# A two-block transformer kernel: eight-slot ring for expert matrices, one block for router and experts, combine inside the layers

## Chip, cores and metric

The kernel runs on one core of a Trainium2 chip. The metric is the device time of one execution in microseconds. TensorE is the matrix engine, VectorE (DVE), ScalarE (ACT) and GpSimd (POOL) are the others; SyncE (SP) only issues DMAs. Each engine executes its own program in order and the engines meet through semaphores. Everything is computed in float32.

## What is computed

The input is `x` with 512 tokens of 1024 features. The first block is a mixer (dilated attention, retention, gates) and a mixture of 64 experts, of which each token uses two; the second block has two layers of attention, pooling, a gated memory and a feed-forward part. The reference, cut to what the change touches:

```python
def first_block(x, ...):
    h = x
    xn = rms_norm(h, norm_mix_w[0])
    h = h + hybrid_mixer(xn, ...)
    hn = rms_norm(h, norm_moe_w[0])
    h = h + hierarchical_moe(hn, w_group, b_group, w_expert, b_expert, w1, w3, w2)
    return rms_norm(h, norm_final_w)

def hierarchical_moe(x2, ...):
    group_p = softmax(x2 @ w_group + b_group);  g_w, g_idx = top_k(group_p, 1)
    sel = (x2 @ w_expert + b_expert) of the chosen group
    e_w, e_idx = top_k(softmax(sel), 2);  e_w = e_w / sum(e_w)
    gate = g_w * e_w;  eid = g_idx * 8 + e_idx
    # every token and choice is put into a slot of its expert
    hid = silu(xb @ w1[e]) * (xb @ w3[e])         # 1024 -> 512
    y = hid @ w2[e]                               # 512 -> 1024
    return sum over both choices of gate * y

def second_block(x, ...):
    h = layer_norm(x, ln0_g, ln0_b)
    for l in range(2):
        h = layer_norm(ALPHA * h + mix(h), ...)
        h = layer_norm(ALPHA * h + conv_glu_ffn(h), ...)
    return h
```

The matrices w1, w3 and w2 of one expert have 2 MB each, 64 experts 403 MB.

## The kernel before

The program is a row of blocks. A block has one instruction stream per engine, and all engines meet at its end: load of x, norm, mixer, merge, a block that clears semaphores (`give_back`), norm (`norm_block`), router (`router_block`), experts (`moe_block`), combine (`combine_block`), another `give_back`, and the layers (`layers_block`) of the second part. All SBUF memory is one tensor `arena`; `mixer_memory`, `moe_memory` and `layer_memory` lay views of it over one another.

Mixer: SP issues four small table loads (`tables_in`), then nine loads of w_in, three for each of three slots (`sp_first`, L277), each of 512 KB in pieces of 512 bytes, then the attention masks. The first matmul (L328) waits for the three loads of slot 0. POOL waits for `tables_in` and then starts with a memset.

Norm before the experts: SP loads the norm's weights, ACT squares, POOL takes the power, DVE scales, PE transposes (L786), ACT copies to `aT` (L717).

Router: SP loads the router's matrices, biases and four constant tables (L957), with `rw_in` counting all eight; POOL writes 4 MB of zeros to the DRAM buffer `y_slots` (L996), the rows of possible overflow blocks. PE multiplies `aT` with the router matrices (L977, 64 matmuls of 72 columns). DVE then runs a chain of some hundred small instructions, each waiting for the one before, that ends in the slot number `yrel` of each token and choice (L1095), its integer form for the combine (L1098 to L1100), and the number of overflow blocks, which goes to DRAM and back through SP (L967, L969). With these inputs no overflow block is needed.

Experts: each expert has 32 slots for tokens. A loop of 16 turns handles four experts per turn, as two pairs. Six SBUF slots of 2 MB hold w1, w3 of two experts and w2 of two experts. For each pair PE waits for the four up matrices, issues 64 up matmuls (L1183, four at a time in the four column groups), four transposes (L1189), waits for the two w2 and issues 32 down matmuls (L1199). ACT applies silu (L1252) and copies the transposed hidden values (L1254); DVE multiplies (L1304) and copies the result out (L1309); ACT sends it to `y_slots` (L1257). SP fetches the next up matrices after `up_done` (L1137, L1138) and the next w2 after `down_done` (L1143). At the end of each turn PE gathers the tokens of the next four experts by 64 matmuls with a 0/1 matrix `G` (L1165), which DVE has made by comparing `yrel` with a ramp (L1288 twice, then L1294 or L1301), and ACT copies them to `xt` (L1244). The gather is also done after the last turn.

Combine: POOL issues 16 indirect DMAs (L1340), each fetching half a result row (2 KB) for 128 tokens and one of their two choices; DVE adds each, times the gate, to `h` (L1353). After `give_back` the layers begin: SP loads weights (L2302 on, L1692), ACT squares `h` (L2329), DVE and POOL make the norm's factor, DVE applies it (L2385), and the second part follows.

## Time and profile before

| | us |
|---|---|
| median of 3 runs | 3744.47 |
| lowest and highest run | 3734.27, 3748.82 |
| profiled execution | 3744.31 |
| its span, first to last instruction | 3742.5 |
| PE busy | 3031.5 (81%) |
| DVE busy | 680.5 (18%) |
| ACT busy | 508.1 (14%) |
| POOL busy | 278.2 (7%) |

Busy PE time is modelled, since matmuls are pipelined, and the granted clock of TensorE changes in the run. The page has the span in 40 equal slices of 93.6 us. The other views are: the waits (who waited for whom), the timeline (instructions in order of time with the idle time ahead of each and what ended it), windows (busy time, granted clock and DMA of a stretch), and the DMA view (packets and bytes of each queue).

### The profile page before, as it was taken

The page shows a single profiled execution, that of the slowest core. Times are in us where ns is not written, and L with a number is a line of the kernel's source. Part 1 is how long each engine was busy: PE and PEld are TensorE (multiplying, and loading weights), DVE is VectorE, ACT ScalarE, POOL GpSimd, SP SyncE. Part 2 cuts the span into 40 slices and gives each one's busy share as a digit, 9 for nine tenths or more (in the row PEclk, how much of TensorE's full clock was granted, in tenths as well). Part 3 has the DMA queues.
Part 4 walks back from the last instruction along what each step waited for, and adds up shares of the span by engine and source line. Part 5 has one row for each costly group of instructions (what it writes and reads, how often), then busy time and mean ns, then how long its engine had stood idle before and what let it go on. Part 6 is the DMA issues. An engine that isn't in the chain of part 4 may idle for free. (4 is left out here: it accounts for less than half of the span.)

```text
span 3742.5 us, 30146 instructions
## 1 busy us (share of the span) xinstructions
PE 3031.5 (81%) x12308; PEld 1589.1 (42%) x12308; DVE 680.5 (18%) x1742; ACT 508.1 (14%) x1001; POOL 278.2 (7%) x283
## 2 busy tenths in 40 slices
PE   6999999999645555545455559899999998999999
PEld 4666665544531222212122235444444554444443
DVE  1222222201120100000010032331110222321102
ACT  1222242210100000000000021310000113210000
POOL 1000003211000000000000040020000200020000
PEclk9999999999857778777787779999999998999999
DMA  5111111113149999999999841112312111032220
GB/s 151 51 34 51 34 35 51 57 34 101 58 172 394 388 387 395 389 391 398 395 386 387 344 149 59 57 45 68 101 68 79 58 69 57 5 98 89 68 90 34
DMA packets 193092, 587.06 MB, mean 157 GB/s; under 512 B 16994, under 2 KB 143202, under 8 KB 168162
## 3 DMA queue, kind: packets, MB, share of 16 engines
q1 hardware_dynamic: 186066, 568.93, 39.6%
q0 software_dynamic: 2320, 8.39, 0.7%
q10 hardware_dynamic: 4608, 8.39, 0.6%
q8 instruction: 67, 1.10, 0.1%
q14 instruction: 31, 0.25, 0.0%
HBM read 571.00 MB, written 14.68 MB: 156 GB/s over the span
## 5 line engine op out<-in xcount | busy, mean ns | idle before, releaser
L1183 PE MATMUL bank<-arena 128*32 128x512 f32 x2048 | 297.5, 745 | 416.6 <-DMA arena<-in_moe_w 416.6
L2238 PE MATMUL bank<-arena 128*128 128x512 f32 (+2 forms) x1472 | 608.6, 576 | 9.1 <-DVE arena L1627 9.1
L328 PE MATMUL bank<-arena 128*128 128x384 f32 x1280 | 431.1, 489 | 14.5 <-DMA arena<-in_w_in 14.5
L2238 PEld LDWEIGHTS bank<-arena 128*128 128x128 f32 x1472 | 275.9, 191 | 339.8 <-issue 329.7
L1183 PEld LDWEIGHTS bank<-arena 128*32 128x32 f32 x2048 | 81.5, 133 | 621.1 <-issue 621.1
L328 PEld LDWEIGHTS bank<-arena 128*128 128x128 f32 x1280 | 237.4, 190 | 175.5 <-DMA arena<-in_w_in 14.8
L2247 PE MATMUL bank<-arena 128*128 128x512 f32 x704 | 303.2, 592 | 0.0
L1741 PE MATMUL bank<-arena 128*128 128x512 f32 (+3 forms) x736 | 249.7, 499 | 0.0
L2247 PEld LDWEIGHTS bank<-arena 128*128 128x128 f32 x704 | 133.0, 189 | 168.4 <-issue 168.4
L1741 PEld LDWEIGHTS bank<-arena 128*128 128x128 f32 x736 | 139.1, 190 | 104.1 <-issue 72.6
L1304 DVE TENSOR_TENSOR arena<-bank,arena 64x512 f32<-64x512 f32 x32 | 32.8, 1026 | 689.3 <-ACT arena L1252 689.3
L1165 PE MATMUL bank<-arena 128*128 128x128 f32 x1088 | 128.6, 279 | 25.0 <-DVE arena L1294 25.0
L1199 PE MATMUL bank<-arena 128*32 128x512 f32 x1024 | 130.6, 655 | 15.2 <-ACT arena L1254 15.2
L1165 PEld LDWEIGHTS bank<-arena 128*128 128x128 f32 x1088 | 125.4, 195 | 38.6 <-DVE arena L1294 25.2
L1252 ACT ACTIVATE arena<-bank 64x512 f32<-64x512 f32 x32 | 18.9, 591 | 750.5 <-PE bank L1183 750.5
L1916 PE MATMUL bank<-arena 128*128 128x512 f32 x256 | 111.4, 592 | 0.0
L325 PE MATMUL bank<-arena 128*128 128x512 f32 x256 | 110.9, 593 | 0.0
L2289 DVE TENSOR_SCALAR arena<-arena 128x512 f32<-128x512 f32 x44 | 25.3, 574 | 457.9 <-ACT arena L2275 457.9
L1340 POOL DMA_INDIRECT arena<-y_slots,arena x16 | 17.4, 1090 | 1136.9 <-PEq L1334 1132.3
L2275 ACT ACTIVATE arena<-bank 128x512 f32<-128x512 f32 x44 | 26.3, 598 | 522.9 <-PE bank L2238 522.9
L389 PE MATMUL bank<-arena 128*128 128x64 f32 x640 | 81.0, 275 | 12.3 <-ACT arena L453 12.3
L1661 POOL TENSOR_TENSOR arena<-arena 128x1 f32<-128x1 f32 x20 | 13.0, 648 | 995.7 <-DVE arena L1639 995.7
(304 smaller groups left out, 2676.0 us busy)
## 6 DMA issues: line engine op xcount, KB each, us to landing
arena<-in_moe_w SPq DMA_DIRECT2D x192, 2048.0 KB, 19.0
arena<-in_w_up SPq DMA_DIRECT2D x44, 1024.0 KB, 7.7
arena<-in_w_in SPq DMA_DIRECT2D x52, 512.0 KB, 5.6
arena<-in_w_down SPq DMA_DIRECT2D x10, 2048.0 KB, 7.7
arena<-in_w_in SPq DMA_DIRECT2D x12, 1024.0 KB, 5.2
y_slots<-arena ACTq DMA_DIRECT2D x32, 256.0 KB, 9.9
arena<-in_w_in SPq DMA_DIRECT2D x4, 2048.0 KB, 9.8
arena<-in_w_out SPq DMA_DIRECT2D x4, 2048.0 KB, 7.8
```

The lines of the kernel that those rows point to most:

```text
L325: ins = pe.matmul(banks[s % 2][:, :], w[:, k, tile(b)], m.aT[:, k, :], start=(k == 0), stop=(k == KT - 1))
L328: ins = pe.matmul(banks[s % 2][:, 0:CW], m.aT[:, k, tile(t)], w[:, k, :], start=(k == 0), stop=(k == KT - 1))
L389: ins = pe.matmul(banks[2][:, 256:256 + HD], m.pt[:, tile(4 * i + j)], m.v[q % 2][:, k, g, HD * hh:HD * hh + HD], start=(i == 0 and j == 0 ...
L1165: ins = pe.matmul(banks[5 + d // 4][:, tile(d % 4)], m.hn[:, t, tile(d)], m.G[:, t, :], start=(t == 0), stop=(t == T - 1))
L1183: ins = pe.matmul(banks[pr][q:q + CAP, :], m.xt[:, k, c:c + CAP], up_dst(2 * e2 + up)[:, k, :], start=(k == 0), stop=(k == KT - 1))
L1199: ins = pe.matmul(banks[3 + pr][q:q + CAP, :], m.ht[:, f, CAP * e2:CAP * e2 + CAP], down_dst(4 + e2)[:, f, 512 * half:512 * half + 512], s ...
L1304: dve.tensor_tensor(by_place(m.hid[0:64, :], FF // P), spread(banks[pr][64:128, :], FF // P), spread(m.hs[64:128, :], FF // P), ALU.mult)\
L1741: ins = pe.matmul(out, a, b, start=(i == 0), stop=(i == len(terms) - 1))
L1916: ins = pe.matmul(banks[2 * t + half][:, :], m.mixT[:, k, tile(t)], slot_view(m, i)[:, k, :], start=(first and k == ks[0]), stop=(last and ...
L2238: ins = pe.matmul(banks[2 * (j % 2) + half][:, part], w[:, k, c0:c0 + P], m.aT[:, k, part], start=(k == 0), stop=(k == KT - 1))
L2247: ins = pe.matmul(banks[2 * t + half][:, :], m.hidT[:, k, tile(t)], v[:, k % 4, 512 * half:512 * half + 512], start=(k == 0), stop=(k == N ...
L2275: act.activation(m.gp[j % 2][:, 2:], banks[2 * (j % 2) + 1][:, :], ACT.Copy).then_inc(G["f_gcopy"], 1)
```

## The change

1. `y_slots` is laid out in rows of 1024 values, one row per slot, instead of two rows of 512. The write of 4 MB of zeros moves from the router block to the start of `pool_mixer`, behind the wait for `tables_in`; POOL's first write into the zero source later waits for it.
2. Both `give_back` blocks go. The mixer's semaphores are cleared by POOL inside the expert block; those of router, experts and combine are kept to the end.
3. In the norm block before the experts SP issues, behind the norm's weights, the eight router loads and then eight expert fetches. The norm's scratch memory moves to where `G`, `xt`, `hs`, `hid`, `ht` and `yo` lie.
4. Router and experts become one block. DVE makes the first `G` directly after `yrel` and its integer form, and the overflow count after that. SP doesn't wait for the count's return from DRAM before the loop.
5. The six expert slots become a ring of eight; fetch number x + 8 goes out when fetch x has been used: in each pair after `up_done` four, after `down_done` two. A turn of the loop covers eight experts (seven turns, and the last eight experts written out). The gather for the next four experts stands between the up matmuls and the transposes of each second pair; there is none after the last pair.
6. The combine moves into the layers' block: eight indirect DMAs of 4 KB rows at the start of `pool_layers`, eight additions at the start of `dve_layers`; ACT's square of a tile waits for its two additions. The layer's views of memory are rearranged so that SP's loads don't touch the gathered rows.
7. `gate` and `yidx_i` join the persistent views, so later views move by 64 bytes.

The diff, cut to its core (waits and loop bodies that are the same are left out):

```diff
-def pool_mixer(nc, pool, A, m, G):
+def pool_mixer(nc, pool, A, m, G, y_slots):
     need = Need(pool)
+    zero = m.rn2.rearrange("p a b -> p (a b)")
+    pool.memset(zero, 0.0).then_inc(G["zero_ready"], 1)
+    pool.wait_ge(G["zero_ready"], 1)
+    pool.dma_start(y_slots[MAIN * CAP:, :].rearrange("(p a) (h n) -> p (a h) n", p=P, h=2),
+                   zero.unsqueeze(1).broadcast_to([P, MORE * CAP // P * 2, 512])).then_inc(G["y_zeroed"], 16)
...
@@ norm_block, sync
             sp.dma_start(m.nw, w.partition_broadcast(P)).then_inc(G["norm_w_in"], 16)
+            if further:
+                further(sp)
...
+def load_expert(sp, m, G, A, at, i):
+    pp, j = at // 6, at % 6
+    e = 8 * i + 2 * pp + (j // 2 if j < 4 else j - 4)
+    sp.dma_start(m.w[at % WSLOT], expert_src(A, PARTS[j], e)).then_inc(G[f"e_in{at % WSLOT}"], 16)
+
+def loads_of_router(sp, m, G, A):
...
+    for at in range(WSLOT):
+        load_expert(sp, m, G, A, at, 0)
+
+def sp_moe(sp, m, G, A, eb_dram):
...
+    def loads(i, n):
+        for x in range(n):
+            pp, j = x // 6, x % 6
+            sp.wait_ge(G["up_done" if j < 4 else "down_done"], 4 * i + pp + 1)
+            load_expert(sp, m, G, A, x + WSLOT, i)
+
+    with sp.Fori(0, NIT - 1) as i:
+        loads(i, 24)
+    loads(NIT - 1, 24 - WSLOT)
...
+    def pair(i, pp, last):
...
+        ins.then_inc(G["up_done"], 1)
+        if pr and not last:
+            pe.wait_ge(G["g_ready"], 2 * i + h + 2)
+            gather()
+        pe.wait_ge(G["hid_ready"], 4 * i + pp + 1)
...
+def pool_moe(pool, m, G, cleared):
+    pool.memset(m.hid, 0.0).then_inc(G["zeroed"], 1)
+    for n in cleared:
+        pool.sem_clear(G[n])
...
+    do(dve.tensor_copy(m.yidx_i, m.yrel))
...
+    picks(P, 0)
+    dve.tensor_tensor(m.G, m.G, m.G1, ALU.add).then_inc(G["g_ready"], 1)
+    do(dve.tensor_scalar(m.e64[4], m.e64[2], m.piota, None, ALU.is_le))
...
-def combine_block(nc, m, G, banks, y_slots):
-            for n in range(16):
-                k, half, t = n % 2, n // 2 % 2, n // 4
...
@@ act_layers
     for t in range(T):
+        ln("combined", 2 * t + 2)
         act.activation(m.z[:, t, :], m.h[:, t, :], ACT.Square, accum_out=m.nss[:, t:t + 1]).then_inc(G["n_sq"], 1)
...
+def pool_layers(pool, m, G, y_slots):
     ln = Need2(pool, G)
+    for n in range(2 * T):
+        pool.indirect_dma_start(
+            out=m.yg[n], out_offset=None, in_=y_slots,
+            in_offset=bass.IndirectOffsetOnAxis(ap=m.yidx_i[:, n % 2, n // 2:n // 2 + 1], axis=0))\
+            .then_inc(G[f"y_in{n}"], 16)
...
@@ dve_layers
+    for t in range(T):
+        for k in range(2):
+            ln(f"y_in{2 * t + k}", 16)
+            n = dve.scalar_tensor_tensor(m.h[:, t, :], m.yg[2 * t + k], m.gate[:, k, t:t + 1], m.h[:, t, :],
+                                         ALU.mult, ALU.add)
+            n.then_inc(G["combined"], 1)
+            ln("combined", 2 * t + k + 1)
```

## Rows read from the trace of the kernel before

**Rows 1.** The page's slices of the whole span: bytes moved, GB/s.

```profile
GB/s 151 51 34 51 34 35 51 57 34 101 58 172 394 388 387 395 389 391 398 395 386 387 344 149 59 57 45 68 101 68 79 58 69 57 5 98 89 68 90 34
```

**Rows 2.** Waits of 1087.07 to 2139.6: us in total, times, longest us.

```profile
PE bank L1183 <- DMA arena<-in_moe_w: 416.6, 32, 17.3
```

**Rows 3.** Windows: us, busy PE, PEld, DVE, ACT, POOL, clock, DMA share, GB/s.

```profile
1087.07:2139.60 1052.53, 564.59 (x4188) 243.59 (x4188) 89.66 (x129) 70.00 (x110) 0.00 (x0) 0.77 0.94 390
1555.00:1580.00 25.00, 17.02 (x140) 9.83 (x136) 2.85 (x5) 2.48 (x3) 0.00 (x0) 0.86 1.01 430
1547.00:1549.50 2.50, 2.04 (x20) 0.40 (x12) 0.00 (x0) 0.39 (x1) 0.00 (x0) 1.00 0.07 26
1020.00:1022.00 2.00, 0.38 (x4) 0.14 (x2) 0.00 (x0) 1.73 (x4) 0.67 (x2) 1.00 0.00 0
1038.00:1048.00 10.00, 10.00 (x49) 10.00 (x48) 0.70 (x3) 0.00 (x0) 0.00 (x0) 0.50 0.00 0
```

**Rows 4.** Timeline in the loop: start us, us, engine, line, operation, tiles.

```profile
1518.29 3.64 PE L1199 MATMUL bank<-arena 128*32 128x512 f32 x32 [0.47 <-ACT arena L1254]
...
1539.06 9.99 PE L1183 MATMUL bank<-arena 128*32 128x512 f32 x64 [17.13 <-DMA arena<-in_moe_w]
...
1557.11 7.41 PE L1165 MATMUL bank<-arena 128*128 128x128 f32 x64
```

**Rows 5.** Timeline from the end of the merge to the first gather.

```profile
1003.96 0.42 DVE L886 TENSOR_TENSOR arena<-arena,bank 128x256 f32<-128x256 f32 x1 [3.04 <-PE bank L859]
1008.09 0.34 SPq L702 DMA_DIRECT2D arena<-in_norm_moe_w  x1
...
1021.34 1.28 ACT L1004 ACT_TABLE_LOAD   x1 [0.27 <-PEq L698]
...
1034.33 13.93 PE L977 MATMUL bank<-arena 128*128 128x72 f32 x64 [13.95 <-DMA arena<-in_consts]
...
1077.61 0.17 DVE L1095 SCALAR_TENSOR_TENSOR arena<-arena 128x8 f32<-128x8 f32 x1
...
1086.83 1.30 DVE L1288 TENSOR_TENSOR arena<-arena 128x512 f32<-128x512 f32 x2 [6.90 <-PEq L952]
1087.07 0.39 SPq L1137 DMA_DIRECT2D arena<-in_moe_w  x1
...
1088.91 10.01 PE L1165 MATMUL bank<-arena 128*128 128x128 f32 x64 [25.04 <-DVE arena L1294]
```

**Rows 6.** DMA queues of 1027.1 to 1033.1: packets, MB, share of the engines.

```profile
q0 software_dynamic: 563, 2.31, 93.5%
q1 hardware_dynamic: 491, 0.17, 10.7%
```

**Rows 7.** Timeline of mixer start and zero write; last, the DMA queue, 30 to 35.

```profile
29.66 0.10 POOL L588 MEMSET arena<- 128x1 f32 x1 [11.60 <-DMA arena<-in_consts]
...
35.06 12.88 PE L328 MATMUL bank<-arena 128*128 128x384 f32 x32 [14.53 <-DMA arena<-in_w_in]
...
1022.64 1.43 POOL L996 DMA_DIRECT2D y_slots<-arena  x1 [0.32 <-POOL arena L994]
...
q1 hardware_dynamic: 2878, 1.45, 117.4%
```

**Rows 8.** Timeline from the last result to the final norm.

```profile
2147.43 0.34 ACTq L1257 DMA_DIRECT2D y_slots<-arena  x1
...
2153.88 0.60 ACT L1244 ACTIVATE arena<-bank 128x512 f32<-128x512 f32 x1 [2.97 <-PE bank L1165]
...
2156.41 1.05 POOL L1340 DMA_INDIRECT arena<-y_slots,arena  x1 [1132.35 <-PEq L1334]
...
2159.93 0.75 DVE L1353 SCALAR_TENSOR_TENSOR arena<-arena 128x512 f32<-128x512 f32 x1 [12.66 <-DMA arena<-y_slots,arena]
...
2177.29 1.14 POOL L1340 DMA_INDIRECT arena<-y_slots,arena  x1 [0.30 <-issue]
...
2191.45 1.28 DVE L2385 SCALAR_TENSOR_TENSOR arena<-arena 128x1024 f32<-128x1024 f32 x1
```

More of the change, by code:

```diff
@@ L950, in router_block, with load @@
+def loads_of_router(sp, m, G, A):
     cols, _ = const_columns()
     consts = A["consts"]
+    def load(dst, src):
+        sp.dma_start(dst, src, allow_slow_non_contiguous=True).then_inc(G["rw_in"], 16)
+    load(m.rw[:, :, 0:NG], A["moe_w_group"][0].rearrange("(p k) n -> p k n", k=KT))
+    load(m.rw[:, :, NG:], A["moe_w_expert"][0].rearrange("(p k) n -> p k n", k=KT))
+    load(m.rb[:, 0:NG], A["moe_b_group"][0].partition_broadcast(P))
+    load(m.rb[:, NG:], A["moe_b_expert"][0].partition_broadcast(P))
+    for dst, name in ((m.iota, "iota"), (m.before, "before"), (m.ones, "ones"), (m.piota, "piota")):
+        load(dst, consts[:, cols[name][0]:cols[name][0] + cols[name][1]])
+    for at in range(WSLOT):
+        load_expert(sp, m, G, A, at, 0)
@@ L963, in _ @@
-            for dst, name in ((m.iota, "iota"), (m.before, "before"), (m.ones, "ones"), (m.piota, "piota")):
-                load(dst, consts[:, cols[name][0]:cols[name][0] + cols[name][1]])
-            sp.wait_ge(G["routed"], 1)
-            sp.dma_start(eb_dram.rearrange("a b -> b a"), m.misc_i[0:MORE, 0:1]).then_inc(G["eb_sent"], 16)
-            sp.wait_ge(G["eb_sent"], 16)
-            sp.dma_start(m.eb_i[0:1, :], eb_dram).then_inc(G["eb_in"], 16)
-            sp.wait_ge(G["eb_in"], 16)
+            sp_moe(sp, m, G, A, eb_dram)
@@ L972, in _ @@
         @block.tensor
         def _(pe):
-            pe.wait_ge(G["rw_in"], 128)
-            for t in range(T):
-                for k in range(KT):
-                    ins = pe.matmul(banks[t][:, 0:NG + NE], m.aT[:, k, tile(t)], m.rw[:, k, :],
-                                    start=(k == 0), stop=(k == KT - 1))
-                ins.then_inc(G["logits_done"], 1)
-            pe.wait_ge(G["assigned"], 1)
-            for t in range(T):
-                for u in range(t + 1):
-                    pe.matmul(banks[4][:, t * NE:(t + 1) * NE], m.ones if u < t else m.before,
-                              m.both[:, u, :], start=(u == 0), stop=(u == t))
@@ L986, in _ @@
-            for u in range(T):
-                ins = pe.matmul(banks[5][:, 0:NE], m.ones, m.both[:, u, :], start=(u == 0), stop=(u == T - 1))
-            ins.then_inc(G["counted"], 1)
+            pe_moe(pe, m, G, banks)
+        @block.scalar
+        def _(act):
+            act_moe(act, m, G, banks, y_slots)
         @block.gpsimd
         def _(pool):
-            pool.memset(m.hid, 0.0).then_inc(G["zeroed"], 1)
-            pool.memset(m.zero, 0.0).then_inc(G["zeroed"], 1)
-            pool.wait_ge(G["zeroed"], 2)
@@ L1028, in _ @@
-            dve.wait_ge(G["rw_in"], 128)
-            for t in range(T):
-                dve.wait_ge(G["logits_done"], t + 1)
-                ins = dve.tensor_tensor(m.lg[:, t, :], banks[t][:, 0:NG + NE], m.rb, ALU.add)
-                step(ins)
-            step.wait(T)
-            gl = m.lg[:, :, 0:NG]
-            gmax, gidx, gw = m.r1[0], m.r1[1], m.r1[4]
-            first(gl, gmax, m.r8[2], gidx, m.r8[3])
-            step(dve.tensor_tensor(m.r8[0], gl, over(gmax, 8), ALU.subtract))
-            step.wait(step.n)
@@ L1332, in combine_block @@
[L1332 to L1354 removed]
+            dve_moe(dve, m, G, banks)
@@ L2444, with program @@
 INPUTS = None
-def program(nc, A, outs, stop=None, start=0):
+def program(nc, A, outs):
     ctx = ExitStack()
@@ new lines, in program @@
+        own = take(nc, G, MIXER_SEMS + MERGE_SEMS)
+        m = mixer_memory(arena)
+        norm_views(m, m.ring_at)
+        load_x(nc, m, G, A)
+        norm_block(nc, m, G, banks, 0, "rms", m.ns, A["norm_mix_w"][0])
+        mixer_block(nc, m, G, banks, A, y_slots)
+        merge_block(nc, m, G, banks, A)
+        m = moe_memory(arena)
+        for n in ROUTER_SEMS + MOE_SEMS + COMB_SEMS:
+            G[n] = ctx.enter_context(nc.semaphore(n))
+        eb_dram = nc.dram_tensor("further_experts", (1, MORE), i32, kind="Internal").ap()
@@ L2484, in program @@
+        norm_block(nc, m, G, banks, 1, "rms", m.hn, A["norm_moe_w"][0], runs=True,
+                   further=lambda sp: loads_of_router(sp, m, G, A))
+        moe_block(nc, m, G, banks, A, eb_dram, y_slots, own[1])
+        own[0].close()
         m = layer_memory(arena)
@@ L2496, in take @@
     return own, names
-def give_back(nc, G, taken):
-    own, names = taken
-    with nc.Block() as block:
-        @block.gpsimd
-        def _(pool):
-            for n in names:
-                pool.sem_clear(G[n])
-    own.close()
 def load_x(nc, m, G, A):
```

711 lines of the change are left out of this document (333 added, 378 removed).

## The prediction, made before the changed kernel was run

> **What bounds the kernel now.** I read the page's slices first: for ten of the forty slices (13 to 22) the data rate stands near 390 GB/s and is far lower elsewhere [rows 1]. That plateau is the expert loop. The waits of that stretch say why: the up matmuls (L1183) waited 416.6 us for expert matrices, 32 times, once per pair of experts, and nothing else in the loop makes TensorE wait as long [rows 2]. So the loop goes at the pace of the fetches, 13 us of wait per pair. Then I asked whether the fetches run flat out. Over the whole stretch they move 390 GB/s at a DMA share of 0.94; in the 25 us from 1555 to 1580 they move 430 GB/s at a share of 1.01; at 1547.0 to 1549.5 only 26 GB/s at 0.07 [rows 3]. The timeline places that hole: it lies just ahead of the end of an up group (1539.06 to 1549.05) [rows 4], for the four up slots are given back only there, and with six slots just two fetches (the w2 pair) are queued meanwhile. Two fetches at 430 GB/s last 9.8 us, the up group 10.0 us, and SP's issue and the start of the transfer come on top: the queue runs dry once per pair. Ahead of the loop the trace shows 83 us from the merge's last add (1004.38) to the first expert fetch (1087.07) in which no expert matrix moves [rows 5]. Everything before and after is a fixed chain that the change touches only at its seams.
>
> **Part 1: mixer start (adds).** The 4 MB of zeros now leave POOL after `tables_in`, which in this trace is 29.66 us, 5.4 us before the first w_in matmul starts (35.06, waiting for its three 512 KB loads) [rows 7]. Memset and issue put the first zero packets near 33.6 (0.9 us for memset and hand-over, then 3.1 us: the same write is issued at 1022.64 and I read its first traffic near 1025.8, an estimate). How do two queues share? In 1027.1 to 1033.1, 563 zero packets of 4 KB went with 491 small ones on SP's queue: about one for one, so the small ones crept at 82 per us [rows 6], where alone they go at 2878 in 5 us, 576 per us [rows 7]. The zeros need some 11 us. If the last 430 packets of w_in's first slot remain at 33.6, the ramp lets them through in about 2 us; with 1000 left they would take 9 us more. I take +1.5 us there and +1 us for the second slot, which is needed 12.9 us later: **+2.5 us**, bounds 0 and +9; I stay near the low end because the zeros begin only 1.5 us before the landing. POOL's own 2 us cost nothing: its next work waits for products of the first matmuls; without that cover they would show in full.
>
> **Part 2: seams before the router (removes).** The merge's last add ends at 1004.38 and the norm starts at 1008.09: 3.7 us of semaphore clearing, against 0.27 us at an ordinary block change (the ACT row at 1021.34) [rows 5]. The clearing moves to POOL inside the expert block, where POOL has nothing else to do. **-3.4 us.** The norm itself is unchanged: SP's new issues (8 router loads and 8 fetches, some 10 us) are behind its own weight load and end before the norm does. If SP were held by a full queue the block's end would wait for it; six fetches in flight never held it, so I cost it at nothing.
>
> **Part 3: the router's start.** Its first matmul waited until 1034.33 for `consts`, whose small packets were starved by the zeros as above [rows 5, 6]. Now these loads are issued during the norm, 7 us or more before use, with no zeros about: start at 1021.4, **-13.0 us**. The expert fetches queue behind them and don't delay them.
> Then the clock. Those 64 matmuls took 13.93 us at a granted clock of 0.50 [rows 3, 5]; the same number of 128-row loads and matmuls in the gather takes 7.41 us when the clock is at its upper level [rows 4]. At 1020 to 1022 the granted clock is 1.00, raised by the norm's transposes [rows 3], and now the router follows within half a microsecond instead of 14. I take 7.4 us: **-6.5 us**, bounds 0 (clock falls all the same) and -6.5.
>
> **Part 4: from slots to gather.** `yrel` is done at 1077.78, the gather's first matmul is at 1088.91: 11.1 us for four index operations, the overflow tail, a DRAM round trip and a block change. Now one cast (0.2 us) and the picks (1086.83 to 1088.91, 2.1 us) stand between [rows 5]: **-8.8 us**. The round trip stays on SP's queue ahead of its loop; it is over some 6 us after the picks, the first slot comes free only 18 us after them, so it is covered.
>
> **Part 5: the loop.** Counting from the first gather matmul G (1088.91 now), today's last fetch ends at 2139.6: G + 1050.7. After: gather 10.0 us [rows 5], copy 0.6, up group at the upper clock 7.3 (twice the 3.64 us that 32 such matmuls take) [rows 4], so slots come free at G + 18. By then all eight are filled: 16.8 MB at 428 GB/s are 39 us, begun at about 1015 in today's times, and G falls near 1060. What is left is 184 fetches, 30.67 pairs. Is the queue always full with eight slots? At the landing of a pair's last up matrix four fetches are outstanding (its w2 pair and the next pair's first two), 19.6 us of work; the up group needs 10 us, and at half clock throughout 14.6 us (twice 7.3). The next two come with the down matmuls, 13 to 14 us after up in an odd pair, since a gather (7.41) now stands between. The queue never empties. So a pair costs 12.58 MB of matrices and 0.26 MB of results, 12.85 MB at 428 GB/s (426 to 430): 30.0 us, against 32.9 now. 30.67 x 30.0 = 920 us, and 1.7 us until the first data flow: last fetch at G + 939.8. **-110.9 us**; 29.9 to 30.15 us per pair give or take 4.5 us.
> Moving the gather ahead of the transposes costs nothing in a fetch-bound loop: it hides DVE's and ACT's hidden-layer steps. If that cover were gone, 7.4 us per four experts would show.
> The Trainium skill speaks against this part: "DMA: Bandwidth & Descriptors", section "Where 436 GB/s comes from", says that for transfers between HBM and SBUF the memory side binds at about 358 GB/s per core. By that rule no ring could beat today's 390, and a pair would cost 35.9 us. The trace disagrees, with 390 over 1052 us and 430 while the queue is full [rows 3].
>
> **Part 6: end of the loop.** Today the last result is sent at 2147.43, ACT's last and useless xt copy ends at 2154.48, and the combine begins at 2156.41 [rows 8]. Without that gather the end hangs on the write's landing (estimate 2.5 us; a gather lands 3.5 us after its issue) plus the same 1.9 us: 4.4 instead of 9.0, **-4.6 us**.
>
> **Part 7: combine.** From the first gather to the first final-norm product (L2385) pass 35.0 us today: 16 gathers and sums, semaphore clearing, four squares [rows 8]. After: eight gathers of the same 4.2 MB, eight sums of 1.3 us hidden under them, squares hidden but the last. Paced by issue alone (20.9 us for 15 steps, 1.4 us each) the sum is 3.5 to the first landing, 7 x 1.4, 1.3 for the last sum and 1.7 for its square and power: 16.3 us. But SP now sends the layer's loads at once, 8 MB and more on the same engines. Their mixed packets should run between the 291 GB/s of 512 byte packets [rows 7] and 430 [rows 3], say 356 in all (an estimate); if the gathers' long packets get two thirds, one takes 2.2 us, and if half, 2.95 us. That gives 4.3 + 7 x 2.2 + 3.0 = 22.7 us, or 27.9 us. I take 22.7: **-12.3 us**, bounds -18.7 and -7.1. The layer's own loads land later than today relative to the block's start, but their first reader comes 12 us after L2385, behind the gathers' end.
>
> **Sum.** 2.5 - 3.4 - 13.0 - 6.5 - 8.8 - 110.9 - 4.6 - 12.3 = -157.0 us. The profiled execution took 3744.3 us (span 3742.5), within 0.2 us of the median 3744.47; I predict 3744.3 - 157.0 = **3587.3 us**.
>
> **Rivals.**
> A. *The queue still runs dry.* Were fetches bound by something other than free slots (issue, or the descriptors in flight), a pair would stay at 32.9 us: 30.67 x 2.9 = +89, giving 3676 (half of it would be 3632). Against it: with work queued the rate is 430 for 25 us on end [rows 3].
> B. *TensorE becomes the bound* because its clock stays at the lower level: at half clock throughout, two pairs need (by doubling the times at the upper clock, transposes and hand-overs included) about 65 us, 32.6 each: +80, giving 3667. Against it: each up group lifts the clock midway.
> C. *A deeper queue reads slower, and the kernel ends slower than before.* A full queue is no promise of a rate: w_in's loads keep every engine busy (share 117.4%) and move 291 GB/s [rows 7]. If expert fetches, with eight in flight, fell to that, a pair would cost 44.2 us: +435, giving 4022. It decides below 366 GB/s, where the 394 MB left take 1077 us and eat every gain. Against it: those packets are 512 bytes and expert fetches go in long ones, at 430 with all six slots in flight [rows 3].
> D. *The ring's doubled loop body doesn't stay loaded.* The Trainium skill ("Runtime: NRT & Kernel Launch", "Instruction fetch mechanics") says that a taken branch to code outside the loaded window stalls for a fetch. No row here prices it; seven jumps back meet a wait of 13 us per pair today [rows 2], so it would not change the sum.
>
> **Chances.** Forecast 0.82, A (in part or whole) 0.10, B 0.04, C 0.02, within 0.5% of before 0.02. The bounds of the parts add up to 3575 and 3610; the runs of before spread by 14 us, and a partial A reaches further up: **3570 to 3620**. A measurement tells about 0.5% (19 us) from no change. Faster 0.96, same 0.02, slower 0.02.
>
> **What would show it.** The w_in wait ends at 36 to 37, not 44. The router's matmuls start within 1 us of the norm, 64 in about 7.4 us. Between the first up groups DMA share is 1.0 and pairs come each 30.0 us; the windows show no hole. TensorE's wait for in_moe_w falls to some 300 to 350 us. The combine's eight gathers take 15 to 18 us beside the layer's loads. The prediction fails if a hole per pair stays, or if the rate with a full queue is under 420.

## The result, and the profile after

The changed kernel takes 3716.72 us (median of 6 runs, 3711.62 to 3722.82), the kernel before 3743.76 (6 runs, 3734.27 to 3748.82). The ratio is 0.9931, 95% interval 0.9915 to 0.9947: 27 us faster, where 157 were forecast. The profiled execution of the changed kernel took 3711.62 us, span 3709.8.

The page of the changed kernel: moved bytes in the 40 slices, the queue that carries the results (packets, MB, share of 16 engines), and the group of the up matmuls (busy us, mean ns | idle before, releaser). It answers to [rows 1] and [rows 2].

```profile
GB/s 197 52 34 52 35 35 51 46 46 91 99 310 410 380 394 358 373 354 400 332 378 395 305 164 49 57 46 68 102 68 78 60 70 57 21 93 80 70 89 34
...
q10 hardware_dynamic: 4160, 8.39, 0.6%
...
L1068 PE MATMUL bank<-arena 128*32 128x512 f32 x2048 | 261.4, 668 | 218.2 <-DMA arena<-in_moe_w 217.3
```

The plateau is no higher than before, and it is uneven. The waits of the loop, 1067 to 2123 (us in total, times, longest us), answer to [rows 2]:

```profile
DVE arena L1324 <- DMA y_slots<-arena: 743.7, 26, 37.7
ACT arena L1156 <- DVE arena L1324: 461.5, 14, 37.8
...
PE bank L1077 <- DVE arena L1319: 286.6, 24, 28.4
...
PE bank L1068 <- DMA arena<-in_moe_w: 217.3, 20, 18.2
```

TensorE's wait for matrices fell as hoped, from 416.6 to 217.3 us, but another stands in its place: DVE waited 743.7 us until an earlier result had left its buffer, ACT waited behind DVE, and TensorE behind both. The timeline shows one case (start us, us, engine, line, operation, in brackets the idle time before and its releaser):

```profile
1505.79 0.54 ACTq L1162 DMA_DIRECT2D y_slots<-arena  x1
...
1542.10 0.69 DVE L1324 COPY arena<-bank 128x512 f32<-128x512 f32 x1 [32.22 <-DMA y_slots<-arena]
...
1542.96 0.53 ACTq L1162 DMA_DIRECT2D y_slots<-arena  x1
...
1582.43 0.69 DVE L1324 COPY arena<-bank 128x512 f32<-128x512 f32 x1 [36.22 <-DMA y_slots<-arena]
```

Results leave at 1505.79, 1542.96 and again only about 40 us later. There are two result buffers, so the copy at 1582.43 waited for the result that was issued at 1505.79: it landed some 77 us after its issue, and the landings of two results are some 40 us apart. Before, a result landed 9.9 us after its issue (median), with the same 256 KB:

```profile
y_slots<-arena ACTq DMA_DIRECT2D x32, 256.0 KB, 9.9
```

The windows (us, busy PE, PEld, DVE, ACT, POOL, clock, DMA share, GB/s), the first over all up groups, the second over the combine, answer to [rows 3]:

```profile
1067.24:2122.00 1054.76, 534.45 (x4124) 234.60 (x4124) 84.45 (x120) 55.29 (x99) 0.00 (x0) 0.76 0.89 373
...
2145.80:2169.90 24.10, 0.00 (x0) 0.00 (x0) 10.66 (x13) 4.60 (x8) 9.32 (x11) 0.50 1.00 357
```

The loop as a whole moves 373 GB/s at a DMA share of 0.89, less than the 390 at 0.94 of [rows 3]. The first up group starts at 1067.24 and the last, the 32nd, at 2113.78: 33.76 us per pair, where the kernel before had 32.90 (its 32 result writes run from 1127.4 to 2147.4). This mean holds one short interval. The ring is full when the loop starts, so the second up group follows the first after 20 us (1087.14); the other thirty intervals average 34.22 us.

Around the loop things went as forecast. The seams before it, which answer to [rows 5] and [rows 7]:

```profile
35.44 13.41 PE L330 MATMUL bank<-arena 128*128 128x384 f32 x32 [14.15 <-DMA arena<-in_w_in]
...
1002.68 0.42 DVE L897 TENSOR_TENSOR arena<-arena,bank 128x256 f32<-128x256 f32 x1 [3.04 <-PE bank L870]
1003.37 0.34 SPq L711 DMA_DIRECT2D arena<-in_norm_moe_w  x1
...
1009.48 4.23 SPq L983 DMA_DIRECT2D arena<-in_moe_w  x8
...
1016.96 3.20 PE L1035 MATMUL bank<-arena 128*128 128x72 f32 x27 [0.99 <-PEq L707]
```

And those behind it, which answer to [rows 8]:

```profile
2136.01 0.52 ACTq L1162 DMA_DIRECT2D y_slots<-arena  x1
2145.83 1.13 POOL L2372 DMA_INDIRECT arena<-y_slots,arena  x1 [1128.39 <-POOLq L1353]
...
2154.10 1.28 DVE L2407 SCALAR_TENSOR_TENSOR arena<-arena 128x1024 f32<-128x1024 f32 x1 [18.12 <-DMA arena<-y_slots,arena]
...
2169.87 1.28 DVE L2418 SCALAR_TENSOR_TENSOR arena<-arena 128x1024 f32<-128x1024 f32 x1
```

The queue's packets hold the clue. A result is 128 packets of 2 KB, so 32 results are 4096 packets. Before, q10 showed 4608 packets, 512 more, or 16 per write; after, 4160, which is 64 more, or 2 per write. The line of the kernel before:

```profile
q10 hardware_dynamic: 4608, 8.39, 0.6%
```

I read the surplus as one closing semaphore packet from each DMA engine that takes part: sixteen before, two after. The reason would be the target's shape. The write's `.rearrange("r (h c) -> h r c", h=2)` puts a dimension of size 2 outermost; the write before was plain rows. The Trainium skill states this rule in "DMA: Bandwidth & Descriptors", section "Why a DMA increments its semaphore by 16 and not by 1": the number of engines is the largest one up to 16 that divides the slowest dimension of both sides. By that rule the changed write runs on two engines, and the packets agree (64 = 32 x 2).

### The profile page after: what moved, and what is told of

Same layout as the page of the kernel before. It is cut to its first block and busy times, and to the rows that moved or that the text cites. A ratio compares the mean times of both kernels' runs of the same rounds, so it can differ in the third digit from the quotient of the medians.

```text
span 3709.8 us, 29704 instructions
## 1 busy us (share of the span) xinstructions
PE 2985.8 (80%) x12244; PEld 1569.5 (42%) x12244; DVE 676.1 (18%) x1727; ACT 493.5 (13%) x990; POOL 269.6 (7%) x275
## 3 DMA queue, kind: packets, MB, share of 16 engines
q10 hardware_dynamic: 4160, 8.39, 0.6%
## 5 line engine op out<-in xcount | busy, mean ns | idle before, releaser
L1068 PE MATMUL bank<-arena 128*32 128x512 f32 x2048 | 261.4, 668 | 218.2 <-DMA arena<-in_moe_w 217.3
L2258 PEld LDWEIGHTS bank<-arena 128*128 128x128 f32 x1472 | 276.0, 191 | 339.7 <-issue 329.6
L330 PEld LDWEIGHTS bank<-arena 128*128 128x128 f32 x1280 | 237.8, 190 | 175.3 <-DMA arena<-in_w_in 14.4
L1077 PE MATMUL bank<-arena 128*128 128x128 f32 x128 | 27.9, 357 | 292.6 <-DVE arena L1319 292.6
L2267 PEld LDWEIGHTS bank<-arena 128*128 128x128 f32 x704 | 133.1, 189 | 168.4 <-issue 168.4
L1761 PEld LDWEIGHTS bank<-arena 128*128 128x128 f32 x736 | 138.9, 190 | 103.8 <-issue 72.1
L1324 DVE COPY arena<-bank 128x512 f32<-128x512 f32 x32 | 22.2, 693 | 814.9 <-DMA y_slots<-arena 777.0
L1087 PE MATMUL bank<-arena 128*32 128x512 f32 x1024 | 144.9, 717 | 16.9 <-ACT arena L1160 16.9
L1077 PEld LDWEIGHTS bank<-arena 128*128 128x128 f32 x128 | 18.5, 179 | 309.5 <-DVE arena L1319 309.5
L1053 PE MATMUL bank<-arena 128*128 128x128 f32 x1024 | 121.2, 280 | 16.3 <-DVE arena L1299 16.3
L1053 PEld LDWEIGHTS bank<-arena 128*128 128x128 f32 x1024 | 118.2, 195 | 29.1 <-DVE arena L1299 16.5
L391 PE MATMUL bank<-arena 128*128 128x64 f32 x640 | 81.0, 275 | 12.3 <-ACT arena L455 12.3
```

Source lines behind the costliest of these rows:

```text
L330: ins = pe.matmul(banks[s % 2][:, 0:CW], m.aT[:, k, tile(t)], w[:, k, :], start=(k == 0), stop=(k == KT - 1))
L391: ins = pe.matmul(banks[2][:, 256:256 + HD], m.pt[:, tile(4 * i + j)], m.v[q % 2][:, k, g, HD * hh:HD * hh + HD], start=(i == 0 and j == 0 ...
L1053: ins = pe.matmul(banks[5 + d // 4][:, tile(d % 4)], m.hn[:, t, tile(d)], m.G[:, t, :], start=(t == 0), stop=(t == T - 1))
L1068: ins = pe.matmul(banks[pr][q:q + CAP, :], m.xt[:, k, c:c + CAP], up_view(m, slots[2 * e2 + up])[:, k, :], start=(k == 0), stop=(k == KT - 1))
L1077: ins = pe.transpose(banks[2][:, tile(f)], m.hid[:, tile(f)], m.ident)
L1087: ins = pe.matmul(banks[3 + pr][q:q + CAP, :], m.ht[:, f, CAP * e2:CAP * e2 + CAP], down_view(m, slots[4 + e2])[:, f, 512 * half:512 * hal ...
```

## The experiments

The theories at first: **A**, the two engines that carry the results also carry a sixteenth each of every fetch, and a fetch ends with its busiest engine; **W**, the loop waits because a result buffer comes free late; **R**, a deeper queue reads more slowly in itself.

**All sixteen engines for the results.** Each result goes out in two transfers without the leading 2 (the semaphore counts double along with it):

```diff
-            act.dma_start(y_slots[bass.ds(8 * CAP * i + 2 * CAP * pp, 2 * CAP), :]
-                          .rearrange("r (h c) -> h r c", h=2), m.yo[pr])\
-               .then_inc(G[f"y_sent{pr}"], 16)
+            for half in range(2):
+                act.dma_start(y_slots[bass.ds(8 * CAP * i + 2 * CAP * pp, 2 * CAP), 512 * half:512 * half + 512],
+                    m.yo[pr][64 * half:64 * half + 64, :])\
+                   .then_inc(G[f"y_sent{pr}"], 16)
```

> The changed kernel with each 256 KB result write issued as two DMAs of 64 rows of 2 KB, nothing else changed. In the changed kernel every write runs on two DMA engines (2 semaphore packets per write in place of 16) and takes some 40 us; here each part should run on all 16. Theory A (the two engines that carry the writes also carry their share of every fetch, and so set the pace): a pair of experts goes from 33.8 us to 29.3 for the matrices plus 0.6 for the write, 29.9; 31 pairs x 3.9 = -121, about 3590 us. Theory W (the buffer's reuse waits for the late landing, the engines' load does not matter): the landing falls to about 6 us, no wait is left, and the time is the same 3590. Theory R (eight fetches in flight make the reads slower, the write is a bystander): stays at 3700 to 3715.

It took 3603.93 us (3578.67 to 3605.3), ratio 0.96 (0.9552 to 0.9649). Its page (slices, result queue, result writes with their median time to landing) and the window over its up groups:

```profile
GB/s 203 53 36 36 36 53 53 36 59 82 59 215 427 428 428 428 429 428 428 429 428 428 225 72 59 1 94 70 82 78 69 79 35 59 47 70 82 94 70 35
...
q10 hardware_dynamic: 5120, 8.39, 0.6%
...
y_slots<-arena ACTq DMA_DIRECT2D x64, 128.0 KB, 8.4
```
```profile
1068.00:1998.60 930.60, 533.09 (x4120) 232.19 (x4124) 85.29 (x121) 55.31 (x99) 0.00 (x0) 0.80 1.00 424
```

The plateau is flat at 428 GB/s, the DMA share 1.00. 5120 packets are 4096 and 64 x 16. From the first up group (1068.1) to the last (1989.87) a pair takes 29.73 us, against 33.76: 31 x 4.03 = 125 us, nearly all of the 129 that were missing. Here too the first interval is short, as the lines below show; the other thirty average 30.06 us ((1989.87 - 1088.11) / 30), the 30.0 us that the prediction gave a full queue.

```profile
1068.06 7.09 PE L1068 MATMUL bank<-arena 128*32 128x512 f32 x64 [1.00 <-ACT arena L1148]
...
1088.11 9.66 PE L1068 MATMUL bank<-arena 128*32 128x512 f32 x64 [6.43 <-DMA arena<-in_moe_w]
```

R is gone: a full queue of eight slots reads at 428. A and W both fit still.

**Four result buffers instead of two**, with the writes on two engines as in the changed kernel:

```diff
+    m.yo += [Space(arena, m.prod_at + 512 * i)(512) for i in range(2)]
...
-                dve.wait_ge(G[f"y_sent{pr}"], 16 * g + 16)
-                dve.tensor_copy(m.yo[pr], banks[3 + pr][:, :]).then_inc(G["yo_ready"], 1)
+                dve.wait_ge(G[f"y_sent{2 * h + pr}"], 16 * i + 16)
+                dve.tensor_copy(m.yo[2 * h + pr], banks[3 + pr][:, :]).then_inc(G["yo_ready"], 1)
```

> The changed kernel, writes on two engines as they are, with four result buffers and semaphores in place of two (the two further ones lie in scratch memory of the router). Theory A: the engines' load is the same, so the time stays at 3700 to 3715 us, and the waits move to another place. Theory W: with twice the time before a buffer is needed again most of the waits go, 3600 to 3640. Theory R: 3700 to 3715.

3719.7 us (9 runs, 3709.71 to 3732.35), ratio 0.9928 (0.991 to 0.9947), the same as the changed kernel, and 33.73 us per pair (1067.8 to 2113.40). Four buffers gain nothing: the number of buffers doesn't set the pace, and the 743.7 us of DVE's wait, the largest of the loop, were no loss that more buffers could win back. But the run doesn't free the loop of the results. DVE's wait for them is gone, and in its place ACT stands in the issue of the writes (duration ns min/median/max, first and last start; the first line from the changed kernel, the second with four buffers):

```profile
L1162 ACTq DMA_DIRECT2D y_slots<-arena x32: 522/529/1193, 1081.9 to 2136.0; - x32
```
```profile
L1164 ACTq DMA_DIRECT2D y_slots<-arena x32: 522/9429/53333, 1082.5 to 2129.7; - x32
```

So W falls as it stood, with the buffers as its cause, but a wait for slow writes in some other place is not excluded yet. That takes a kernel in which no engine waits for results.

**Two edits that did nothing.** I tried to put the results on four engines, and the kernel before's on two, by splitting the rows in order:

```diff
+                    .rearrange("(a b) c -> a b c", a=4),
```

> As e1_write16, but each of the two DMAs has an outermost dimension of 4 in DRAM, so that it should run on four engines. Theory A: each of these four has 32 packets of 0.08 us more per pair, 29.3 + 2.6 = 31.9 us: 31 x 2.0 = 62 us more than e1_write16, about 3650. Theory W: the write's landing is 32 x (0.61 + 0.08) = 22 us, less than a pair, no wait, so the time of e1_write16, about 3590. Theory R: 3700 to 3715.

> The kernel before (six slots, all as it was) with only the result write given the two-row outermost form of the changed kernel. Theory A: the two engines need 29.3 + 5.1 = 34.4 us per pair instead of the 32.9 us of now, and the holes of the six-slot ring come on top in part: between 3790 and 3880 us. Theory W: the write finds idle stretches once per pair and lands within two pairs, no wait: 3744 us. Theory R: no deep queue here, 3744.

They gave 3591.85 us (ratio 0.9576, 0.953 to 0.9622), as with sixteen engines, and 3746.23 (ratio 1.0001, 0.9981 to 1.0021), as before. The result queue's packets say why, the first line from the kernel meant for four engines, the second from the kernel before meant for two:

```profile
q10 hardware_dynamic: 5120, 8.39, 0.6%
```
```profile
q10 hardware_dynamic: 4608, 8.39, 0.6%
```

16 closing packets per transfer in both. I read it so that rows split in order are one run of rows again by the time the transfer is issued; no view shows that step. So neither is evidence on A; the shape must be one that doesn't merge.

By then I had formed a variant of W, called **Q** below. On each engine a result's packets alternate one for one with the 16 KB fetch packets, so 64 packets per engine need about 40 us, longer than a pair; more buffers don't help, and anything under some 40 packets per engine would be harmless. A predicts otherwise: half the load on an engine costs half as much. The next three kernels take the rows out of order (every fourth, or every second), so that they can't merge. Results then stand in other rows.

**Four engines.**

```diff
+                    .rearrange("(y x) c -> x y c", x=4),
```

> Each half of a result (64 rows of 512 columns) goes out in its own transfer, and the target's rows are taken in an order that doesn't merge (every fourth row), so that the slowest dimension is really 4: results stand in other rows than they should, the work is the same. If the slowest dimension sets the number of engines, the page shows 4 semaphore packets a transfer on the results' queue (4096 + 256 = 4352 packets) and 32 data packets on each of four engines per pair. Theory Q (queue): a result's packets alternate one for one with the 16 KB fetch packets (about 0.69 us a turn) wherever the fetch queue is never empty, so a result takes its packets per engine x 0.69 us, and it costs time only where that is more than a pair's 29.8 us. 32 x 0.69 = 22 us: harmless, about 3600 us, transfers landing in about 22 us. Theory A (load): the engines that carry results also carry a sixteenth of every fetch, and the fetch ends with the busiest engine; half the load on each engine is half the loss: (33.76 - 29.8) / 2 = 2.0 us a pair, 31.8 us, about 3655 to 3670 us.

3658.32 us (3639.1 to 3663.67), ratio 0.9783 (0.9743 to 0.9823).

**Half of each result on sixteen engines, half on two.**

```diff
+                dst = y_slots[bass.ds(8 * CAP * i + 2 * CAP * pp, 2 * CAP), 512 * half:512 * half + 512]
+                act.dma_start(dst.rearrange("(y x) c -> x y c", x=2) if half else dst,
```

> Half 0 of every result goes out over 16 engines, half 1 over two (every second row, so results stand in other rows than they should). The two engines carry 32 + 4 packets of 2 KB per pair, half of what the changed kernel gives them. Queue page: 4096 + 32 x 16 + 32 x 2 = 4672 packets. Theory Q: 36 x 0.69 = 25 us, under a pair's 29.8 us: no loss, about 3600 us. Theory A: the same two engines carry half the surplus: 31.8 us a pair, 3655 to 3670 us.

3659.51 us (3651.64 to 3674.57), ratio 0.9807 (0.9769 to 0.9846).

**The same with twice as many packets of half the size.**

```diff
+                for a in range(0, 512, 256 if half else 512):
+                    b = a + (256 if half else 512)
```

> As the kernel with half of each result on two engines, but that half is sent in two transfers of 256 columns: the same bytes, in twice as many packets of 1 KB, so the two engines carry 64 + 4 packets per pair (results again in other rows than they should). Theory Q, in which a packet of a result waits for one fetch packet however small it is: 68 x 0.65 = 44 us a result, over a pair's time, so that the loop slows as in the changed kernel: 3700 to 3740 us. Theory A, if bytes count: 3655 to 3670 us as with 2 KB packets. If neither packets nor bytes on two engines matter: 3600 us.

3663.24 us (3659.35 to 3673.0), ratio 0.9819 (0.9788 to 0.985).

The result queue of the three, in this order:

```profile
q10 hardware_dynamic: 4352, 8.39, 0.6%
```
```profile
q10 hardware_dynamic: 4672, 8.39, 0.6%
```
```profile
q10 hardware_dynamic: 6784, 8.39, 0.6%
```

The counts are those of 4, of 16 and 2, and of 16, 2 and 2 engines (6784 is 6144 data packets and 32 x 20). All three times lie in A's 3655 to 3670; Q wanted 3600 for the first two and 3700 to 3740 for the third. Some of the fit is luck: the kernel before took 3733.15 us beside these three, 14 us less than beside the first runs, so by their ratios they would have taken 3666 to 3680 there. The pair times carry the verdict: A wanted 31.8 us, Q 29.8 for the first two, and they took 31.62 and 31.93. The third, for which Q wanted results 44 us apart, took 32.03. Q falls. It falls by the waits too. In the loop of the first two TensorE's only long wait is for matrices, neither DVE nor ACT waits for a result (ACT's issues take 1.2 us at most), and a pair still takes 2 us more than with sixteen engines; in that of the third DVE waits again for results (the first line from the kernel with four engines, the second from the one with small packets):

```profile
PE bank L1068 <- DMA arena<-in_moe_w: 405.3, 31, 17.9
```
```profile
DVE arena L1328 <- DMA y_slots<-arena: 324.8, 20, 37.4
```

That is 325 us of wait, and the time is that of the kernel with none of it to within 4 us. The waits are there, but they only say which engine stands still while the loop is held to a pace that something else sets. The changed kernel shows it in the small as well. Its results leave 40 us apart for several turns, and then one follows after 12 to 25 us, so that the mean stays at a pair's 34 us: the write that lags behind the fetches for a while catches up when TensorE has stood still and fewer fetches are queued (this last is argued, not measured).

That pace can be worked out. Per pair each of 16 engines carries a sixteenth of six 2 MB matrices, 768 KiB, and the busiest its part of the 256 KiB of results. With 784 KiB a pair took 29.73 us, so an engine needs 0.0379 us per KiB. Pair times are from the start of the first up group to that of the last, over 31:

| results on | KiB on the busiest engine | x 0.0379 us | measured, us |
|---|---|---|---|
| 16 engines | 784 | (29.73) | 29.73 |
| 4 | 832 | 31.5 | 31.62 |
| half on 16, half on 2 | 840 | 31.9 | 31.93 |
| the same, 1 KB packets | 840 | 31.9 | 32.03 |
| 2 (the changed kernel) | 896 | 34.0 | 33.76 |
| 2, four buffers | 896 | 34.0 | 33.73 |

One figure, taken from the first row, gives the others to 0.3 us. Without the short first interval the pair times are 30.06, 32.01, 32.33, 32.43, 34.22 and 34.19 us, the figure is 0.0383 us per KiB, and it gives the others to 0.2 us. The DMA share agrees, though it is a mean and no view shows single engines. If two engines work all the time and fourteen carry 768 of 896 KiB, the mean is (2 + 14 x 768/896)/16 = 0.875, and the window of the changed kernel shows 0.89; with four engines at 832 it is (4 + 12 x 768/832)/16 = 0.94, and the window over that kernel's up groups shows 0.95:

```profile
1067.60:2056.40 988.80, 538.31 (x4121) 233.18 (x4124) 85.22 (x121) 55.21 (x99) 0.00 (x0) 0.78 0.95 399
```

**The kernel before with its results on two engines** asks whether the narrow write costs as much where the queue has holes.

```diff
-                    act.dma_start(y_rows[bass.ds(256 * i + 128 * pr, 128), :], m.yo[pr])\
+                    act.dma_start(y_rows[bass.ds(256 * i + 128 * pr, 128), :].rearrange("(y x) c -> x y c", x=2), m.yo[pr])\
```

> The kernel before (six slots) with every second row of a result's target taken first, so that its write goes out on two engines instead of sixteen (results stand in other rows than they should; the queue page should show 4096 + 64 = 4160 packets). The runs so far say that an engine's work sets the pace: 48 fetch packets of 16 KB per pair at 0.611 us are 29.3 us, and 64 packets of 2 KB cost 4.0 us more (33.76 us a pair against 29.8). In the kernel before a pair takes 32.9 us because the fetch queue runs dry. Theory A1: the two engines work through the others' dry time, so a pair takes what their work needs, 29.3 + 4.0 = 33.3 us, up to 34.5 us where the dry time doesn't fall right: 3747 to 3800 us. Theory A2: the dry time lies in all engines alike and the 4.0 us come on top: 36.9 us a pair, 3870 us. If the six slots hid the write altogether: 3735 to 3747.

3802.91 us (3797.6 to 3803.44), ratio 1.0156 (1.0127 to 1.0184). The result writes of this kernel (duration ns min/median/max, first and last start):

```profile
L1257 ACTq DMA_DIRECT2D y_slots<-arena x32: 528/529/1167, 1127.9 to 2200.1; - x32
```

Its q10 carried 4160 packets, two closing ones per write. That is 34.59 us per pair against 32.90, the upper end of A1. With the deep ring the narrow write costs 4.0 us of a pair more than the wide one, here 1.7; the rest fits in the time in which the fetch queue is dry. So a kernel with holes in its queue shows less than half of what the same write costs once the ring is deep.

**Six slots with results on sixteen engines** asks what the ring itself is worth.

```diff
-WSLOT = 8
+WSLOT = 6
```

> The changed kernel with each result in two transfers of 64 rows x 512 columns over 16 engines, and a ring of six slots instead of eight, so that six matrices are fetched from the norm on. Theory: the two more slots are what keeps the queue filled, so that with six a pair takes again 32.9 us as in the kernel before, while the earlier first fetches stay: 3578 to 3605 (eight slots) plus 31 x 3.1 = 96 us, about 3675 to 3700 us. Rival: the period of 32.9 us was due to the waits around the router or the engines' order and not to the slots: then 3600 us again.

3676.65 us (3663.59 to 3687.9), ratio 0.9832 (0.9795 to 0.9869); 32.48 us per pair (1068.4 to 2075.31). With eight slots it is 29.73: 31 x 2.75 = 85 us come from the two slots, 10 of them in the first interval (30.3 us against 20.1), for which six slots hold too little. The earlier start and the seams are the rest.

**The layers' loads held back** behind the fifth gather, on top of the write over sixteen engines:

```diff
+    sp.wait_ge(G["y_in5"], 16)
     ln_rows(sp, m, G, A, 0)
```

> The changed kernel with each result written in two transfers of 64 rows x 512 columns (16 engines each), and with SP waiting for the fifth gather's landing before it issues the layers' first loads (the combine's norm rows and w_in). The combine took 24.0 us in the changed kernel where the eight gathers' moving and the adds need 15 to 18; if the 21 us of w_in's issue and its packets beside the gathers are the difference, it takes about 17 us and the whole is 5 to 8 us under the version without the wait (3578 to 3605 there): 3571 to 3598. If the layers then wait for w_in, which now starts about 10 us later, nothing is gained or up to 5 us lost.

3573.42 us (3570.89 to 3581.79), ratio 0.9578 (0.955 to 0.9607). From the first gather to the first final-norm product (line 2420 here) pass 18.1 us (2010.90 to 2029.0) in place of 24.5 (2011.95 to 2036.5) without the wait, and the layers' first matmul (line 1620) starts at 2036.38 in place of 2043.86. The timeline with the wait, first and last gather, first add, and the first of SP's w_in issues, now 11 us long where it was 21.6:

```profile
2010.90 1.13 POOL L2374 DMA_INDIRECT arena<-y_slots,arena  x1 [991.76 <-POOLq L1354]
...
2016.06 1.28 DVE L2409 SCALAR_TENSOR_TENSOR arena<-arena 128x1024 f32<-128x1024 f32 x1 [10.59 <-DMA arena<-y_slots,arena]
...
2020.22 1.11 POOL L2374 DMA_INDIRECT arena<-y_slots,arena  x1 [0.30 <-issue]
...
2024.62 11.13 SPq L1713 DMA_DIRECT2D arena<-in_w_in  x4
```

Whether it reaches the end was asked once more, with both on one chip:

> The changed kernel with each result in two transfers of 64 rows x 512 columns, once more, on the same chip as the version that also holds the layers' loads back, so that the two can be compared. Before: 3603.93 (3578.67 to 3605.3). Expected again 3575 to 3606, ratio to the kernel before 0.956 to 0.963.

> The same with SP waiting for the fifth gather before the layers' first loads. In single profiles the combine took 24.5 us without the wait and 18.1 with it. If these 6.4 us reach the end: 6 us under the version without the wait on the same chip, ratio lower by 0.0017. If the layers wait for the later loads instead (SP's loads end 1 to 2 us later): no difference.

Without the wait 3591.18 us (3576.78 to 3607.05), ratio 0.9594 (0.9567 to 0.962); with it 3585.27 (3581.39 to 3602.26), ratio 0.9582 (0.956 to 0.9604). The medians differ by the 6 us expected, but the intervals overlap and the runs of either spread over 20 us or more, so the gain at the end is open. The gain in the combine is seen in both pairs of traces: 24.5 to 18.1 us above, 24.4 to 19.4 us here (2010.28 to 2034.70, and 2011.51 to 2030.91). Both versions beat the changed kernel and the kernel before.

## Why the prediction was wrong

The predicted time was 129 us too low, and the range, 3570 to 3620, missed 3716.72. Cut at the same points, the two profiled executions compare as follows. The span went from 3742.5 to 3709.8, -32.7 us:

| stretch | forecast | measured |
|---|---|---|
| part 1, start to the merge's last add | +2.5 | -1.3 |
| part 2, merge to norm | -3.4 | -3.4 |
| part 3, norm to router matmuls; their clock | -13.0; -6.5 | -12.7; -6.6 |
| part 4, router matmuls' end to first gather matmul | -8.8 | -8.7 |
| parts 5 and 6, first gather matmul to first DMA gather of the combine | -115.5 | +22.1 |
| part 7, combine | -12.3 | -11.0 |
| layers | 0 | -11.1 |

The loop missed by 137.6 us. Part 1 and the layers came out 15 us lower than forecast, for reasons that the prediction didn't have, and that luck hid some of the miss.

**Part 1.** The mixer's first matmul starts at 35.44, not 35.06: +0.4, within the bounds. The whole part, at -1.3, is below them. The 1.7 us between the two lie somewhere in the mixer and weren't followed.

**Parts 2 to 4** held to 0.4 us. Norm and merge are 0.3 us apart (1003.10 to 1003.37), the router starts at 1016.96 at a granted clock of 1.00 and is through its 64 matmuls in 7.34 us, the gather's first matmul is at 1056.22. The clock term was given a bound of nothing, and for a reason: in the profile of the kernel meant for four engines the same 64 matmuls ran at the lower level (1.2 GHz) nearly throughout and took 13.49 us (window from 1017, granted clock 0.53), though the program ahead of them is the same. The kernel with small packets shows it too (13.60 us); in the nine other profiles of the changed kernel and its variants they took 7.33 or 7.34 us. First the window of the changed kernel, then that of the one meant for four engines:

```profile
1016.96:1024.30 7.34, 7.34 (x64) 7.19 (x64) 0.70 (x3) 1.25 (x1) 0.49 (x1) 1.00 1.01 429
```
```profile
1017.00:1031.00 14.00, 13.49 (x64) 13.32 (x64) 0.86 (x4) 1.29 (x2) 0.53 (x1) 0.53 1.00 428
```

**Part 5** is where it failed, and in one step: "12.58 MB of matrices and 0.26 MB of results, 12.85 MB at 428 GB/s (426 to 430): 30.0 us". The results' bytes were spread over sixteen engines without looking at the shape of their write, which stood in the full diff (the cut shown above leaves it out). On two engines the same 0.26 MB cost 4.0 us of a pair more than on sixteen. The rest of the part is right once that is mended: with results over sixteen engines 949.6 us pass from the first gather matmul to the last result's issue (1056.96 to 2006.55), where 947.6 were forecast (939.8 to the last fetch, and 7.8 from there that the prediction left as they were); a pair takes 30.06 us once the ring that was full at the start is used up, the rate is 424 over the loop, TensorE waits 352 us for matrices (300 to 350 were forecast), and the queue does not run dry. The Trainium skill's 358 GB/s for the memory side ("DMA: Bandwidth & Descriptors", section "Where 436 GB/s comes from"), which spoke against the part, did not bind here: the loop moved 424 GB/s over 930 us. The prediction read it without its condition, for the same page, in its section "Bandwidth", ties the figure to both cores of a memory pair streaming at once. The rule that would have told, on how many engines a transfer uses, is in the same page and was not weighed.

**Part 6** reckoned with 4.4 us from the last result's issue to the combine; it is 9.8 in the changed kernel (2136.01 to 2145.83), for the last write too drains through two engines. With sixteen it is 5.4 (from 2006.55, the first of the two issues, to 2011.95).

**Part 7**: 24.0 us against 22.7. The window's 357 GB/s meets the estimate of 356; SP's issue of w_in took over 21 us beside the gathers.

**Layers.** The prediction costs them at nothing and they lost 11.1 us (1551.0 to 1539.9) with no edit in them. They differ that much from run to run: with results on sixteen engines one profile has 1565.1 us from the first final-norm product to the end, at a mean granted clock of 0.96, another of the same program 1540.4 at 0.98. The kernel before had 1551.05 at 0.97, the changed one 1539.93 at 0.98 (windows, same columns, in this order):

```profile
2036.50:3601.60 1565.10, 1494.94 (x4232) 740.69 (x4232) 350.72 (x787) 211.23 (x454) 127.97 (x119) 0.96 0.20 66
```
```profile
2034.70:3575.10 1540.40, 1470.30 (x4232) 728.25 (x4232) 349.99 (x787) 211.18 (x454) 127.78 (x119) 0.98 0.20 67
```
```profile
2191.45:3742.50 1551.05, 1480.15 (x4232) 733.17 (x4232) 350.85 (x787) 211.26 (x454) 127.33 (x117) 0.97 0.20 69
```
```profile
2169.87:3709.80 1539.93, 1469.84 (x4232) 728.32 (x4232) 350.55 (x787) 211.03 (x454) 128.16 (x119) 0.98 0.20 67
```

TensorE's busy time for the same 4232 matmuls differs by nearly as much as the windows do; what sets the clock in a run is open. The spread of 25 us is half as wide as the range that was given, and the range had no term for it. With it in mind the mended kernel's 3603.93 and 3591.18 stand well beside the forecast of 3587.3.

**Rivals.** A (the queue runs dry, 3676) came nearest in time, and half of it is what happened: a DMA share of 0.89 fits fourteen engines that run dry for part of each pair, though not for want of slots but because two others were never done. B (TensorE's clock) didn't occur: the clock is 0.76 in the changed loop and 0.80 with the write mended, and neither is what TensorE waits for. C (deep queue reads slower) is refuted by 428 GB/s. D (instruction fetch) shows no stall: with the write mended the thirty intervals behind the first average 30.06 us, jumps included. The mechanism that decided stood in none of them: it was neither the fetches nor TensorE but the one transfer whose shape the change rewrote.

## What to carry to other kernels

When the diff changes a transfer's access pattern, work out how many engines it will run on before counting its bytes, and count load per engine, not in total: with every engine full of long fetches, a small write on two of them costs what half its bytes take at one engine's rate, here 2% of the traffic and 12% of the loop's time. Closing packets in the queue's count (packets less data packets, by transfers) read it off the page in one division. And the largest wait in the table need not be the cause: more buffers took nothing off the time, while a split of the write took off 125 us.

## What the runs showed of the hardware

- Sixteen engines sustain 424 to 428 GB/s for 930 us on one core with up to eight 2 MB reads queued; six slots gave 390 in the kernel before and 389 in the changed one.
- The write on two engines drains at about 0.62 us per 2 KB packet beside the fetches (64 packets per engine in the 39.5 us from 1542.96 to 1582.43), eight times what 2 KiB x 0.0379 us would be: about one 16 KB fetch packet (16 KiB x 0.0379 = 0.61 us) passes for each. Results then land some 40 us apart, yet over the loop the pace follows the bytes.
- Halving the packets to 1 KB at the same bytes changed a pair by 0.1 us (31.93 to 32.03).
- A split of the rows that stays in order changed nothing in the number of engines (4608 and 5120 packets, 16 closing ones per transfer); one that reorders rows did (4352 packets, 4 per transfer).
